# Two more projection parts computed as pairs of products, and another order of the first products of the program

## The reference: what is computed

```python
h = rms_norm(x, norm_mix_pre[l])
u = h @ w_in                                  # 1024 -> 6484 columns
(z, xs, bs, cs, dt_raw, fq, fk, fv, ff, mq, mk, mv, dq, dk, dv, iq, ik, iw) = split(u)
y_ssm  = mamba2_branch(z, xs, bs, cs, dt_raw, ...)   # conv, silu, state scores with decay
y_fox  = fox_branch(fq, fk, fv, ff, fox_fbias)       # attention with forget gates
y_moba = moba_branch(rope(mq), rope(mk), mv)
y_dsa  = dsa_branch(rope(dq), rope(dk), dv, rope(iq), rope(ik), iw)
gates  = sigmoid(h @ w_gate + b_gate)
merged = sum_n gates[n] * (y[n] @ w_branch[n])
x = x + rms_norm(merged @ w_out, norm_mix_post[l])
x = x + rms_norm(swiglu(rms_norm(x, norm_ffn_pre[l])), norm_ffn_post[l])
```

## Time and profile before

| | us |
|---|---|
| time, median of 3 runs | 2176.01 (2175.82 to 2176.3) |
| time of the profiled execution | 2175.88 |
| its span in the trace | 2174.0 |
| TensorE busy | 2157.4 (99%) |
| VectorE busy | 1487.8 (68%) |
| ScalarE busy | 1118.6 (51%) |

### The profile page before, as it was taken

One profiled execution on the slowest core, in us unless ns is written; L12 is line 12 of the kernel. 1 busy time (PEld: TensorE's weight loads), 2 busy tenths in 40 slices (PEclk: granted clock), 3 DMA queues, 4 the chain that ended last, 5 costly groups with the idle time before them and its releaser, 6 DMA issues.

```text
span 2174.0 us, 30972 instructions
## 1 busy us (share of the span) xinstructions
PE 2157.4 (99%) x13072; PEld 1852.7 (85%) x13072; DVE 1487.8 (68%) x1660; ACT 1118.6 (51%) x1413; POOL 44.7 (2%) x46
## 2 busy tenths in 40 slices
PE   8999999999999999999999999999999999999998
PEld 7988888888988888888898888988889888898887
DVE  6788677655778868666678777456557877745654
ACT  5555555454565564545466535444446653544442
POOL 0000000000000000000000100000000010000000
PEclk9999999999999999999999999999999999999999
DMA  8555564655664556556564444456566444545652
GB/s 278 167 167 176 168 232 160 208 197 168 198 186 155 162 204 203 177 190 214 161 197 135 143 150 162 150 170 192 191 171 204 134 143 151 160 151 169 193 192 76
DMA packets 248751, 380.75 MB, mean 175 GB/s; under 512 B 22495, under 2 KB 158693, under 8 KB 248614
## 3 DMA queue, kind: packets, MB, share of 16 engines
q1 hardware_dynamic: 248614, 378.78, 54.2%
HBM read 372.26 MB, written 1.05 MB: 172 GB/s over the span
## 4 chain that ended last, share of the span: by engine, by line
PE 97%; DVE 2%; ACT 1%; issue 1%; DMA 0%; POOL 0%; DVEq 0%; SPq 0%; POOLq 0%; ACTq 0%
PE ps L666 9%; PE ps L2567 8%; PE ps L803 8%; PE ps L3137 8%; PE ps L2471 7%; PE ps L2518 5%; PE ps L1135 5%; PE ps L2492 5%; PE ps L670 5%; PE ps L656 5%; PE ps L2625 4%; PE ps L1038 4%; PE ps L2494 2%; PE ps L762 2%; PE ps L1056 2%; PE ps L2588 2%
## 5 line engine op out<-in xcount | busy, mean ns | idle before, releaser
L3498 DVE TENSOR_TENSOR b_wlo<-b_ring,b_whi 128x2048 fp32r<-128x2048 f32 (+2 forms) x168 | 379.4, 2262 | 107.8 <-ACT b_whi L3162 107.1
L1444 DVE TENSOR_TENSOR a_wlo<-a_ring,a_whi 128x2048 fp32r<-128x2048 f32 (+1 forms) x173 | 392.8, 2273 | 56.9 <-ACT a_whi L1161 56.5
L3162 ACT CAST b_whi<-b_ring 128x2048 fp32r<-128x2048 f32 (+2 forms) x168 | 318.1, 1893 | 202.2 <-PE ps L3137 76.0
L1161 ACT CAST a_whi<-a_ring 128x2048 fp32r<-128x2048 f32 (+1 forms) x173 | 329.0, 1903 | 150.1 <-PE ps L1038 45.2
L666 PE MATMUL ps<-a_nsp,a_whi 128*128 128x512 f32 x864 | 218.4, 394 | 0.0
L666 PEld LDWEIGHTS ps<-a_nsp,a_whi 128*128 128x128 f32 x864 | 155.2, 189 | 27.9
L2567 PE MATMUL ps<-b_whi,b_nsp 128*128 128x512 f32 x512 | 170.9, 400 | 0.0
L803 PE MATMUL ps<-a_whi,a_nsp 128*128 128x512 f32 x512 | 162.3, 392 | 0.0
L670 PEld LDWEIGHTS ps<-a_nsp,a_wlo 128*128 128x128 f32 x864 | 117.8, 190 | 8.5
L670 PE MATMUL ps<-a_nsp,a_wlo 128*128 128x256 f32 x864 | 120.4, 282 | 0.0
L2567 PEld LDWEIGHTS ps<-b_whi,b_nsp 128*128 128x128 f32 x512 | 96.1, 188 | 20.9
(11 more groups left out here) (614 smaller groups left out, 4426.2 us busy)
## 6 DMA issues: line engine op xcount, KB each, us to landing
a_ring<-in_w_in SPq DMA_DIRECT2D x49, 1024.0 KB, 5.4
b_ring<-in_w_in SPq DMA_DIRECT2D x46, 1024.0 KB, 5.1
a_ring<-in_w_ffn_in SPq DMA_DIRECT2D x44, 1024.0 KB, 5.1
a_ring<-in_w_gate SPq DMA_DIRECT2D x32, 1024.0 KB, 5.4
b_ring<-in_w_up SPq DMA_DIRECT2D x32, 1024.0 KB, 5.5
b_ring<-in_w_down SPq DMA_DIRECT2D x32, 1024.0 KB, 4.9
a_ring<-in_w_ffn_out SPq DMA_DIRECT2D x22, 1024.0 KB, 5.0
a_ring<-in_w_branch SPq DMA_DIRECT2D x16, 1024.0 KB, 5.1
```

The lines of the kernel that those rows point to most:

```text
L1161: nc.scalar.copy(high(l, h), raw(l, h)).then_inc(hi_ok, 1)
L1444: nc.vector.tensor_tensor(low(l, h), raw(l, h), high(l, h).bitcast(F32), ALU.subtract).then_inc(lo_ok, 1)
L3162: nc.scalar.copy(high(l, h), raw(l, h)).then_inc(hi_ok, 1)
L3498: nc.vector.tensor_tensor(low(l, h), raw(l, h), high(l, h).bitcast(F32), ALU.subtract).then_inc(lo_ok, 1)
```

## The change

Parts 9 (iq, 256 columns) and 12 (the first half of fk) join the paired parts. Their release and the count of their eviction follow from that, and the semaphores that count pairs are others (`sig_ok` and `yl_ok` in place of `spe` and `spv`), with the later waits on these raised by the number of pairs. ScalarE waits before the first half of part 12 for the transposes of the convolved channels. At the program's begin the eight high products of part 2 for tile 0 move ahead, to right behind the turn of tile 1, and its four low products stand behind parts 0 and 1 of tile 1.

```diff
-PAIRED = (10, 11, 13, 14, 15, 16, 21, 22, 23)
+PAIRED = (9, 10, 11, 12, 13, 14, 15, 16, 21, 22, 23)
+N_PAIRS = 2 * len(PAIRED)
...
-    pair_half, pair_sum = spe, spv
+    pair_half, pair_sum = sig_ok, yl_ok
...
-    freed = [(pair_sum, 2 + pairs[key]) if key in pairs else ...
+    freed = [(pair_sum, pairs[key]) if key in pairs else ...
...
-            apart = ((0, 1), (2,))
-            for some in apart:
-                for t in range(NT):
-                    for i in some:
...
+            for t in range(NT):
+                for i in range(2):
...
+                if t == 0:
+                    turn_in(pe.engine, l, 1)
+                    pe.wait_ge(hi_ok, 3)
+                    high_rows(ps[:, 2, :], 2, 0, 0)
+            pe.wait_ge(lo_ok, 3)
+            low_rows(ps[:, 2, :], 2, 0, 0)
+            lead_rows(2, 1).then_inc(half_used, 1)
...
             if i in PAIRED:
+                if i == 12:
+                    act.wait_ge(xs_ps, 1)
                 if i == 22:
                     act.wait_ge(qk_ps, 4)
                 evict_half(i, 0)
```

More of the change, by code:

```diff
@@ L142 @@
     "gpost_in": 64, "par_in": 48, "small_in": 96, "sgw_in": 320,
-    "w_small": 368, "tr_ps": 8, "full": 51, "half_used": 44, "par_ps": 1, "few_ps": 1, "cum_ps": 5, "cb_ps": 1,
+    "w_small": 368, "tr_ps": 8, "full": 53, "half_used": 44, "par_ps": 1, "few_ps": 1, "cum_ps": 5, "cb_ps": 1,
     "xs_ps": 1, "dec_ps": 8, "ix_ps": 1, "y_ps": 1, "qk_ps": 12, "yt_ps": 4, "pt_ps": 6, "o_ps": 6, "pr_ps": 16,
-    "out_used": 3, "mix_ps": 2, "dn_ps": 2, "in_ms": 4, "hi_ok": 87, "nhi_ok": 8, "free_a": 33, "spe": 21,
+    "out_used": 3, "mix_ps": 2, "dn_ps": 2, "in_ms": 4, "hi_ok": 87, "nhi_ok": 8, "free_a": 31, "spe": 3,
     "silu_ok": 2, "cb_ok": 1, "dec_ok": 8, "ix_rl": 1, "ex_ok": 12, "yt_out": 1, "pt_a": 6, "ot_ok": 6,
-    "sig_ok": 4, "yh_ok": 4, "mh_ok": 4, "ssq_ok": 6, "ms_ok": 6, "fg_free": 11, "hh_ok": 11, "xn_ok": 8,
-    "nlo_ok": 8, "lo_ok": 87, "pad_ok": 2, "par_ok": 1, "spv": 20, "lcat_ok": 5, "cum_ok": 2, "free_v": 10,
+    "sig_ok": 26, "yh_ok": 4, "mh_ok": 4, "ssq_ok": 6, "ms_ok": 6, "fg_free": 11, "hh_ok": 11, "xn_ok": 8,
+    "nlo_ok": 8, "lo_ok": 87, "pad_ok": 2, "par_ok": 1, "spv": 2, "lcat_ok": 5, "cum_ok": 2, "free_v": 10,
     "rope_ok": 10, "xs_ok": 1, "sc_ok": 2, "msq_ok": 1, "mx_ok": 12, "yt_ok": 1, "pn_ok": 12, "pt_v": 6,
-    "isc_ok": 1, "pen_ok": 2, "yl_ok": 4, "pr_free": 16, "mg_ok": 14, "ml_ok": 4, "x_ok": 4, "fu_free": 11,
+    "isc_ok": 1, "pen_ok": 2, "yl_ok": 26, "pr_free": 16, "mg_ok": 14, "ml_ok": 4, "x_ok": 4, "fu_free": 11,
     "hs_ok": 11, "in_rs": 2, "rstd_ok": 7
@@ L425, in first_block @@
     pairs = {("in", i, n): 2 * PAIRED.index(i) + n + 1 for i in PAIRED for n in range(2)}
-    freed = [(pair_sum, 2 + pairs[key]) if key in pairs else (free_a, n + 1 - sum(k in pairs for k in order[:n]))
+    freed = [(pair_sum, pairs[key]) if key in pairs else (free_a, n + 1 - sum(k in pairs for k in order[:n]))
              for n, key in enumerate(order)]
@@ L726, in lead @@
                 return
-            apart = ((0, 1), (2,))
-            for some in apart:
-                for t in range(NT):
-                    for i in some:
[L731 to L743, removed]
+            for t in range(NT):
+                for i in range(2):
+                    if t == 0 and i == 0:
+                        pe.wait_for(first_lo, 1)
+                    elif t == 0:
+                        pe.wait_ge(lo_ok, 2)
+                    pe.wait_ge(nlo_ok, 2 * t + i + 1)
+                    mm = lead_rows(i, t)
+                    if i == 1:
+                        mm.then_inc(full, 1)
+                    elif t == 1:
+                        mm.then_inc(half_used, 1)
+                if t == 0:
[5 more added lines that the diff above has]
+            lead_rows(2, 1).then_inc(half_used, 1)
             pe.wait_ge(lo_ok, 4)
@@ L1027, in tensor @@
                 if m == 0:
-                    pe.wait_ge(yl_ok, n + 1)
+                    pe.wait_ge(yl_ok, N_PAIRS + n + 1)
                 if t == 0:
@@ L1514, in convolve @@
             if b % 2 == 0:
-                dve.wait_ge(*freed[unit["in", H_XBC + b // 2, 0]])
+                dve.wait_ge(*freed[unit["in", H_XBC + b // 2, 1 if H_XBC + b // 2 in PAIRED else 0]])
             dve.wait_ge(pad_ok, 1)
@@ L1693, in add_half @@
             out = dst[name][:, at_ + m, :]
-            dve.wait_ge(pair_half, 3 + pairs["in", i, m])
+            dve.wait_ge(pair_half, pairs["in", i, m])
             V.scalar_tensor_tensor(out, ps[:, unit["in", i, m] % 2, SEQ:2 * SEQ], QSCALE.get(name, 1.0), out,
@@ L1706, in gated @@
             if m == 0:
-                dve.wait_ge(sig_ok, n + 1)
+                dve.wait_ge(sig_ok, N_PAIRS + n + 1)
             dve.wait_ge(pr_ps, i + 1)
```

## The result

The changed kernel took 2183.28 us (median of 7 runs, 2181.68 to 2184.8), the kernel before 2176.01 (7 runs, 2175.82 to 2176.3): a ratio of 1.0033, 95% interval 1.0024 to 1.0043. It is slower by 7.3 us, 0.33%; 2181.9 was forecast, with a range from 2178.4 to 2184.3. The profiled execution took 2183.06 us, its span is 2181.2. What the table doesn't say and the list of times does: the runs of before scatter over 0.5 us, those of the changed kernel over 3.1.

A forecast was written before the change was run, and what follows sets the result against it. TensorE, busy 99%, was taken to bound the kernel; two layers at 3.5 us each less 1.1 at the begin gave +5.9 us on 2175.88, and with 0.13 to the median 2181.9 us, range 2178.4 to 2184.3.

The forecast's parts named there:

- TensorE bounds, and a new wait is paid in full: TensorE, busy 99% of the span, sets the time; each us of new wait adds a us, each saved one removes one.
- The saving of a pair: Parts 9 and 12, both layers: each part converted to paired saves 0.18 us of TensorE's products, 0.7 us for all four.
- The 0.04 us by the formula: Parts 9 and 12: saving per converted part by the skill's product step, 0.2 us for all four; measured steps were preferred.
- The begin: Program's begin: part 2's eight high products fill the gap behind tile 1's turn, gaining 0.96 to 1.23 us, taken as 1.1.
- The first wait: Before half 1 of part 10: TensorE waits 2.28 us, until about 74.80, for VectorE's second addition of part 9, each layer.
- The second wait: Before `decay(0)`: TensorE waits 1.7 us for VectorE's `state_inputs`, so `decay(0)` starts at 100.24, 3.41 us later, each layer.
- rival (c): TensorE's clock falls in the new waits, 1.5 us lost at each of four: 2187.9 us; chance 0.05.
- (a): Not slower: VectorE's answers come in time at both places, the waits don't bite, only gains stay: 2174.2 us; chance 0.12.
- (b): Only the wait before half 1 of part 10 occurs; VectorE reaches `state_inputs` sooner than reckoned: 2178.9 us; chance 0.14.
- Rival (d): Larger loss: a table load or a load of weights comes on top, +2 to +3 us: 2184.5 us; chance 0.07.
- The loads behind the copies of part 9: SyncE's queue: part 16's load, issued at 77.47 before, comes some 3 us later, hidden since needed over 30 us later.

The follow-up runs named there:

- closer: The changed kernel with evictions and additions of parts 9, 10 and 12, rotations and `state_inputs` reordered on ScalarE and VectorE against both new waits; 2174.0 us, ratio 0.999.
- the begin alone: The changed kernel with its new order at the program's begin kept, but parts 9 and 12 not paired; 2174.64 us, ratio 0.9995.
- the second wait taken away: The changed kernel with VectorE's rotations ahead of part 12's first addition, `state_inputs` ahead of lo(15) and part 13's addition; 2180.92 us, ratio 1.0025.

## Why the prediction was right, and where not

- **TensorE bounds, and a new wait is paid in full.** Right: the delays of the two layers add up to the difference of the spans, and each wait that was taken away came off the time, less 0.1 to 0.3 us in a layer that the moved instructions cost elsewhere.
- **The saving of a pair, 0.18 us.** Right: part 9 takes 5.59 us in place of 5.76, and the layer of "closer" is shorter by two such savings and 0.14. The 0.04 us by the formula of the Trainium skill (TensorE: Matmul & The Clock Gate, section "Back-to-back issue gap") are not borne out by these rows. That section gives the formula for the gap of an isolated product.
- **The begin, 1.1 us.** Measured 1.23 by the traces and 1.25 by the times of the begin alone; it is the upper bound of the forecast that holds, since the products follow the transposes without their drain.
- **The first wait, until 74.80.** From the first product of part 9 to half 1 of part 10 it forecast 10.65 us (74.80 - 64.15); measured 73.33 - 62.68 = 10.65. Its place, its releaser and what stands before it on VectorE were as written. Taking it out of VectorE's order takes it off the time.
- **The second wait, 1.7 us.** Its idle time is 1.40; `decay(0)` came 3.51 and, without the clock, 3.53 us later for each layer, against 3.5 forecast. Of the difference to 1.7, 0.16 is the drain of the products before it, which the row doesn't count as idle (the next could start at 98.43 + 0.46 = 98.89); by as much again TensorE came later to this place than reckoned. From the end of the first wait to `decay(0)` it is 636.06 - 610.50 = 25.56 us, forecast 100.24 - 74.80 + 0.11 = 25.55.
- **The clock, rival (c), chance 0.05.** This is the step that failed, as a weight and not as a mechanism. The forecast took it as unlikely since no row showed a fall after 0.96 us of idle time; that says nothing of 2.28. Priced at 1.5 us for each fall (measured 1.56), it comes, by the steps of the times, behind the first wait of one of the two layers in 9 of 13 runs, and behind the second wait in no trace. The forecast of 2181.9 is the level with no fall, which 3 of 13 runs had (2181.56 to 2181.68); the median lies one fall higher. With one fall in the sum it would have been 2181.9 + 1.56 = 2183.5.
- **Rivals (a) and (b)** fell with the two rows of waits, which are both there in full. Rival (d) has nothing in the trace either: the table load at 66.08 comes after the eviction of part 9's first half and is over long before the second, and no wait of TensorE for a load is new. The loads behind the copies of part 9 are issued at 79.08 in place of 77.47, that is 3.08 us later against TensorE's own stream, as forecast, and show in no wait.

## What to carry to other kernels

Where TensorE is busy 99% of the time, a change is worth what the other engines' rows of work let it be: before two units share their release with another engine, look at what stands ahead of that release in the engine's own order, and put the release before any long chain that nobody waits for yet. A loss of 7 us and a gain of 2 us differ here only by where a few instructions stand in the rows of ScalarE and VectorE. And price a new wait of TensorE with the clock behind it; when the runs of one kernel fall on separate levels, look at the granted clock behind its longest waits before calling it noise.

## What the runs showed of the hardware

The granted clock of TensorE fell to 0.50 behind a wait with 2.11 us of idle time in some executions and layers and held in others of the same kernel (once in the first trace of the changed kernel, not at all in the second, twice in that with the second wait taken away). Behind 1.4 us idle it fell in none of the eight such waits of four traces, behind 4.32 us in both layers. Each fall cost 1.5 to 1.6 us. At the program's begin, by contrast, the granted clock reads 1.00 while eight transposes take 2.02 us in place of 1.04; in the trace of the kernel before:

```profile
8.50:11.00 2.50, 2.08 (x9) 1.43 (x8) 2.34 (x3) 0.99 (x3) 0.00 (x0) 1.00 1.01 379
```

That column is not to be trusted there.
